# One stage instead of two: merge, output projection, memory keys/values and cross queries

## The chip, the cores and the metric

The kernel runs on one core of one Trainium2 chip. The metric is the device time of one execution in microseconds (us). The kernel before took 2871.36 us (median of 3 runs, 2869.28 to 2875.1). One further execution was taken with the hardware profiler; all rows below are from it.

## The reference, cut to what matters

The reference is one step of a hybrid encoder layer over 1024 prompt tokens and 8 x 16 sample tokens (1152 columns in all, D_MODEL = 1024). The part that is touched:

```python
def rmsnorm(x, g):
    y = x * lax.rsqrt(jnp.mean(x * x, axis=-1, keepdims=True) + 1e-6)
    return y * g

x = x + W_out(sum_b sigmoid(gate_b) * (branch_b @ W_branch_b))     # three branches, 512 -> 1024 each
k, v = split(rmsnorm(mem, norm_mem) @ w_mem_kv, 2)                 # 256 memory rows, 1024 -> 2048
q = rmsnorm(x, norm_x) @ w_xq                                      # 1152 columns, 1024 -> 1024
s = q . k / 16;  x = x + softmax(s) @ v @ w_xo                     # 4 heads of 256
```

Afterwards comes a gated ConvFFN and a final rmsnorm. The memory keys and values (`o_mem`) are outputs too. The RMS factor belongs to a column (a token or a memory row), the gain `g` to a feature, so `(x * g * r) @ W` equals `((x * g) @ W) * r`.

## The kernel before, in words

All activations lie transposed: a feature on a partition, 8 rows of 128 features (`KD`), tokens along the free axis, T = 1152 in three chunks of TC = 384. The program is a chain of stages: in-projection, LRU, RWKV, `stage_merge`, `stage_queries`, `stage_cross`, `stage_tail`. Each is a `with Stage(...)` that owns its buffers, its eight PSUM banks and its semaphores; its exit clears the semaphores and puts a barrier on all engines, so nothing of the next stage starts ahead of it. Within a stage each engine has its own program in a fixed order, written out by hand, and semaphores join them.

**A product** (class `Product`, lines 115 to 307) multiplies by a weight matrix, one tile of 128 output features after another, in pairs (slot `s` = 0, 1). To keep precision each operand is split in a rounded part (`hi`, fp32r) and a rest (`lo`), and three matmuls are added: hi*hi, lo*hi, hi*lo. One tile with 1152 columns is so 8 rows x 3 passes x 3 chunks = 72 matmuls of 384 columns; one of the memory product is 8 x 3 = 24 matmuls of 256 columns. For tile j, SP loads the weights into `raw[s]` once `rest` says that the slot's earlier tile has been split (lines 146, 152). ACT makes `hi` (`split_hi`, L174), which waits for the weights and for `ready` of the tile two before. DVE makes `lo` (`split_lo`, L179). PE runs the tile (L252; the first tile of a product L272) when `lo` is there and the slot's PSUM banks have been emptied (`used`). `pipeline` gives ACT and DVE their order: split of tile 2p, evacuation of tile 2p-1, split of 2p+1, evacuation of 2p. With `after=` the weight buffers are handed from one product to the next; with `next_split` the next product's first two weight tiles are split in the course of this one's last ones. `after_tile=` calls a function on PE behind each tile.

**stage_merge** (L1744): three branch products of half depth (36 matmuls a tile), whose results DVE multiplies with the gates and sums in `xt` (L1853, L1855, L1857); POOL loads the gates (L1792), ACT does the sigmoid (L1820) and rounds the sum (L1814), DVE its rest (L1839). Then `out`, the output projection: SP loads the residual rows into `xt` (L1783) and DVE adds each result to them (L1740). ACT has only the weight splits to do in `out`.

**stage_queries** (L1876): SP loads the memory and the first weights after the barrier. `Norm` (class at L310) of the memory: ACT squares (L342), PE sums over the partitions with a matrix of ones (L365, plain fp32), ACT takes the root (L349), DVE the reciprocal (L372), then for each piece DVE multiplies by gain and factor (L379), ACT rounds (L358), DVE takes the rest (L389). Then `pm`, 16 tiles of K/V, DVE copies them out (L1934). Then the same `Norm` on `xt` in three chunks, and `pq`, 8 tiles of queries; its first tile goes chunk by chunk so as to follow the norm. ACT copies the results out (L1920) and stores them in DRAM (L1922).

**stage_cross** (L1949) begins with 16 transposes of V (L2086) and the load of `q` from DRAM (L1984), for which its first scores (L2024) wait.

Of the kernel before, what the change touches and what calls it, by code (L numbers as in the profile page):

```python
# [26 lines left out]
TC = 384  # L27
# [9 lines left out]
NMEM = 256  # L37
XH, XHD = 4, 256
EPS = 1e-6
GN_EPS = 64e-5  # L40
DEC = float(np.exp(-0.5))

# [44 lines left out]
class Stage:  # L87
# [15 lines left out]
    def sb(self, name, shape, dt=F32):  # L103
        return self.ctx.enter_context(self.nc.sbuf_tensor(f"{self.name}_{name}", shape, dt))
# [10 lines left out]
class Product:  # L115
# [121 lines left out]
    def products(self, pe, x_rest, by_chunk, beside=None, freed=None, after_row=None, after_tile=None):  # L237
# [42 lines left out]
        if after_tile:  # L280
            after_tile(1)
            for p in range(1, self.pairs):
                for s in range(2):
                    tile(p, s, True)
                    after_tile(2 * p + s)
            return
        if not beside:
# [1456 lines left out]
def stage_merge(nc, env, io):  # L1744
# [3 lines left out]
    with Stage(nc, "merge") as st:  # L1748
        banks = st.banks()
        S = st.sem  # L1750
        xt = env["xt"]
        operands = [st.sb(f"operands{i}", [P, KD, T], F32R) for i in range(2)]
        bh, bl = [x[:, 0:KM] for x in operands], [x[:, KM:KD] for x in operands]
        total = xt
        xh, xl = operands[1], st.sb("merged_lo", [P, KD, T], F32R)
        ring = st.sb("branch", [P, 3, T])
        gates = [st.sb(f"gate{s}", [P, T]) for s in range(2)]
        tmp = st.sb("gated", [P, NTC, TC])
# [5 lines left out]
        out = Product(st, "wout", KD, KD // 2, wtile(io["w_out"], KD), xh, xl, banks, bufs=bufs, after=prods[2])  # L1764
        splits = [StreamSplit(st, f"br{n}", lambda k, n=n: io["branch"][n, :, k], bh[n % 2], bl[n % 2], KM, ring) for n in range(3)]
        half = KD // 2
        with nc.Block() as block:
            @block.sync
            def _(sp):
                for n in range(3):  # L1770
                    prods[n].load_first(sp)
                    if n == 0:
                        splits[0].load(sp)
                    if n < 2:
                        if n:
                            sp.wait_ge(prods[0].ready, KD * NTC)
                        sp.wait_ge(splits[n].rest, KM)
# [6 lines left out]
                out.load_rest(sp)  # L1784

            @block.gpsimd
            def _(pool):
                for n in range(3):
                    def load(p, s, wait=True):
                        if wait:  # L1790
                            pool.wait_ge(prods[n].used, (p * 2 + (s - 1)) * NTC)
                        pool.dma_start(gates[s][:], io["z"][bass.ds(p * 2 + (Z_G + n * KD + s), 1)].rearrange("o p t -> (o p) t")).then_inc(S(f"gate_in{n}_{s}"), 16)  # L1792
                    for s in range(2):
                        if n:
                            pool.wait_ge(prods[n - 1].used, (KD - 1 + s) * NTC)
                        load(0, s, False)
                    with pool.Fori(1, half) as p:
                        load(p, 0)
                        load(p, 1)

            @block.scalar
            def _(act):
# [19 lines left out]
                            round_row(p * 2 + (s - 1))  # L1822
                    prods[n].pipeline(act, prods[n].split_hi, gate, next_split=(prods[n + 1] if n < 2 else out).split_hi)
                round_row(KD - 1)
                out.pipeline(act, out.split_hi, lambda p, s: None)

            @block.vector
            def _(dve):
# [38 lines left out]
                out.pipeline(dve, out.split_lo, add_to_residual(dve, out, xt, None))  # L1867

            @block.tensor
            def _(pe):  # L1870
                for n in range(3):
                    prods[n].products(pe, splits[n].rest, False)
                out.products(pe, S("x_rest"), False)


def stage_queries(nc, env, io):  # L1876

    with Stage(nc, "xq") as st:
        banks = st.banks()
        S = st.sem  # L1880
        xt, vec = env["xt"], env["vec"]
        xh, xl = st.sb("xh", [P, KD, T], F32R), st.sb("xl", [P, KD, T], F32R)
        mem = st.sb("mem", [P, KD, NMEM])
        out = [st.sb(f"q{s}", [P, T]) for s in range(2)]
        bufs, nbufs = Product.buffers(st, KD, "w"), Norm.buffers(st, "norm")
        ones = env["mask"]("ones")
        nx = Norm(st, "nx", xt, vec[:, VAT["norm_x"]:], xh, xl, ones, banks, bufs=nbufs)
        nm = Norm(st, "nm", mem, vec[:, VAT["norm_mem"]:], xh, xl, ones, banks, tc=NMEM, ntc=1, bufs=nbufs)
        nx.eps = nm.eps = env["eps"]
        pq = Product(st, "wq", KD, KD // 2, wtile(io["w_xq"], KD), xh, xl, banks, bufs=bufs)  # L1890
        pm = Product(st, "wm", KD, KD, wtile(io["w_mem_kv"], KD), xh, xl, banks[6:8], tc=NMEM, ntc=1, bufs=bufs)
        kv = env["kv"]
        with nc.Block() as block:
            @block.sync
            def _(sp):
                sp.dma_start(mem[:], io["memt"]).then_inc(S("mem_in"), 16)
                pm.load(sp)
                sp.wait_ge(pm.rest, 2 * KD)
                pq.load_first(sp)
                sp.wait_ge(pm.used, 2 * KD)  # L1900
                sp.dma_start(io["o_mem"], kv[:]).then_inc(S("kv_stored"), 16)
                pq.load_rest(sp)
                sp.wait_ge(S("kv_stored"), 16)

            @block.scalar
            def _(act):
                act.wait_ge(S("mem_in"), 16)
                pm.first_splits(act, pm.split_hi)
                nm.scalar(act)
                pm.pipeline(act, pm.split_hi, lambda p, s: None)  # L1910
                act.wait_ge(pm.ready, 2 * KD)
                nx.squares(act, weights=pq)
                nx.roots(act)

                def evac(p, s):
                    if not (isinstance(p, int) and p == 0):
                        act.wait_ge(S(f"q_stored{s}"), p * 16)
                    for c in range(NTC):
                        act.wait_ge(pq.ready, (p * 2 + s) * NTC + (c + 1))
                        act.copy(out[s][:, c * TC:(c + 1) * TC], pq.bank[s][c][:, 0:TC]).then_inc(pq.used, 1)  # L1920
                    act.wait_ge(pq.used, (p * 2 + (s + 1)) * NTC)
                    act.dma_start(io["q"][:, bass.ds(p * 2 + s, 1)].rearrange("p o t -> p (o t)"), out[s][:]).then_inc(S(f"q_stored{s}"), 16)  # L1922
                pq.pipeline(act, pq.split_hi, evac)
                for s in range(2):
                    act.wait_ge(S(f"q_stored{s}"), 16 * pq.pairs)

            @block.vector
            def _(dve):
                pm.first_splits(dve, pm.split_lo)
                nm.vector(dve)  # L1930

                def evac(p, s):
                    dve.wait_ge(pm.ready, p * 2 + (s + 1))
                    dve.tensor_copy(kv[:, bass.ds(p * 2 + s, 1)].rearrange("p o t -> p (o t)"), pm.bank[s][0][:, 0:NMEM]).then_inc(pm.used, 1)  # L1934
                pm.pipeline(dve, pm.split_lo, evac)
                pq.first_splits(dve, pq.split_lo)
                nx.vector(dve)
                pq.pipeline(dve, pq.split_lo, lambda p, s: None)

            @block.tensor  # L1940
            def _(pe):
                nm.tensor(pe)
                pm.products(pe, nm.rest, True)
                pe.wait_ge(nm.rooted, 1)
                nx.tensor(pe)
                pq.products(pe, nx.rest, True)


def stage_cross(nc, env, io):  # L1949
# [576 lines left out]
def hybrid_stream_step(nc, io):  # L2526
    for name, shape in SCRATCH.items():
        io[name] = nc.dram_tensor(f"scratch_{name}", shape, F32, kind="Internal").ap() if name not in io else io[name]
    with ExitStack() as ctx:
# [7 lines left out]
        for stage in (stage_in_projection, stage_lru, stage_rwkv):  # L2537
            stage(nc, env, io)
        env["xt"] = sb("xt", [P, KD, T])
        stage_merge(nc, env, io)  # L2540
        with nc.sbuf_tensor("mem_kv", [P, 2 * KD, NMEM], F32) as kv:
            env["kv"] = kv
            stage_queries(nc, env, io)
            stage_cross(nc, env, io)
        stage_tail(nc, env, io)


# [75 lines left out]
```

## Time and profile before

| what | value |
|---|---|
| median of 3 runs | 2871.36 us |
| the profiled execution, its own time | 2877.42 us |
| its span, first to last instruction | 2875.9 us |
| PE matmul busy | 2592.2 us (90%) |
| DVE busy | 1340.6 us (47%) |
| ACT busy | 745.6 us (26%) |
| POOL busy | 223.1 us (8%) |
| mean granted TensorE clock | 0.946 |

Start of the span is 0. `stage_merge` has its first matmul at 1267.3 us; `out`, its last product, ends with the matmuls that start at 1538.50 us; `stage_queries` lies from there to 1753.7. A profile's busy time of PE counts matmuls that overlap; where the pace matters, the distance of their starts is read. "idle before" in a row is the engine's idle time ahead of the row, with what ended it.

### The profile page before, as it was taken

To read this page: it belongs to the slowest core of one execution; us is meant where nothing else is said; L and a number is where in the kernel's file an instruction comes from. 1 tells how busy PE (TensorE), PEld (TensorE's weight loads), DVE (VectorE), ACT (ScalarE), POOL (GpSimd) and SP (SyncE) were. 2 spreads that over 40 slices of the span, in tenths; PEclk is the share of its full clock that TensorE was granted. 3 is DMA by queue.
4 is the path that set the end of the run, shared out by engine and by line. 5 is a ranking of instruction groups with operands and counts; after the bars stand their busy time and mean duration, and the time that the engine had idled before them with its cause. 6 is when DMAs were issued, how large, how long until landed. Compare 5 with 4: busy or idle time off the path is not lost. (4 is left out here: it accounts for less than half of the span.)

```text
span 2875.9 us, 49184 instructions
## 1 busy us (share of the span) xinstructions
PE 2592.2 (90%) x20376; PEld 2466.1 (86%) x20376; DVE 1340.6 (47%) x2044; ACT 745.6 (26%) x1147; POOL 223.1 (8%) x373
## 2 busy tenths in 40 slices
PE   6999999999648889839997897879999999999996
PEld 4999999999537778729997696779999999989995
DVE  5102334431566777434723612435665556553256
ACT  4111122221434444123412422323111111111122
POOL 0001110000222233110000000000000000000000
PEclk9999999999759999869998999989999999999998
DMA  3222233322530100034421316431111111123233
GB/s 129 86 85 93 86 104 110 109 96 80 128 127 28 32 23 23 9 127 157 152 96 69 121 71 240 144 130 37 44 47 59 68 68 68 68 97 104 66 95 123
DMA packets 138016, 258.85 MB, mean 90 GB/s; under 512 B 43440, under 2 KB 86240, under 8 KB 135056
## 3 DMA queue, kind: packets, MB, share of 16 engines
q1 hardware_dynamic: 103248, 185.30, 19.3%
q0 software_dynamic: 9168, 37.75, 4.0%
q10 hardware_dynamic: 25472, 33.95, 3.2%
q8 instruction: 98, 1.61, 0.2%
q14 instruction: 30, 0.25, 0.0%
HBM read 190.36 MB, written 67.52 MB: 90 GB/s over the span
## 5 line engine op out<-in xcount | busy, mean ns | idle before, releaser
L252 PE MATMUL tail_bank<-tail_x_hi,tail_w_hi 128*128 128x384 f32 x1494 | 359.7, 340 | 8.2 <-DVE tail_w_lo L179 8.2
L252 PE MATMUL tail_bank<-tail_x_lo,tail_w_hi 128*128 128x384 f32 x1494 | 358.4, 339 | 0.0
L252 PE MATMUL tail_bank<-tail_x_hi,tail_w_lo 128*128 128x384 f32 x1494 | 358.3, 339 | 0.0
L252 PE MATMUL inproj_bank<-inproj_xh,inproj_win_hi 128*128 128x384 f32 x1224 | 283.2, 340 | 0.0
L252 PEld LDWEIGHTS tail_bank<-tail_x_hi,tail_w_hi 128*128 128x128 f32 x1494 | 270.8, 189 | 11.8 <-DVE tail_w_lo L179 11.3
L252 PE MATMUL inproj_bank<-inproj_xl,inproj_win_hi 128*128 128x384 f32 x1224 | 278.8, 336 | 0.0
L252 PE MATMUL inproj_bank<-inproj_xh,inproj_win_lo 128*128 128x384 f32 x1224 | 278.7, 336 | 0.0
L252 PEld LDWEIGHTS tail_bank<-tail_x_hi,tail_w_lo 128*128 128x128 f32 x1494 | 270.9, 189 | 0.0
L252 PEld LDWEIGHTS tail_bank<-tail_x_lo,tail_w_hi 128*128 128x128 f32 x1494 | 270.7, 188 | 0.0
L252 PEld LDWEIGHTS inproj_bank<-inproj_xh,inproj_win_hi 128*128 128x128 f32 x1224 | 216.2, 189 | 2.7 <-issue 2.7
L252 PEld LDWEIGHTS inproj_bank<-inproj_xh,inproj_win_lo 128*128 128x128 f32 x1224 | 218.2, 188 | 0.0
L252 PEld LDWEIGHTS inproj_bank<-inproj_xl,inproj_win_hi 128*128 128x128 f32 x1224 | 218.2, 188 | 0.0
L174 ACT CAST tail_w_hi<-tail_w_raw 128x1024 fp32r<-128x1024 f32 (+2 forms) x100 | 92.6, 926 | 473.7 <-PE tail_bank L252 325.5
L179 DVE TENSOR_TENSOR inproj_win_lo<-inproj_win_raw,inproj_win_hi 128x1024 fp32r<-128x1024 f32 x52 | 63.5, 1224 | 250.1 <-ACT inproj_win_hi L174 250.1
L252 PE MATMUL merge_bank<-merge_operands,merge_w_hi 128*128 128x384 f32 x672 | 143.5, 341 | 13.6 <-DVE merge_w_lo L179 13.6
L2417 DVE TENSOR_TENSOR tail_room<-tail_bank,tail_rs 128x384 f32<-128x384 f32 x132 | 59.6, 507 | 181.7 <-PE tail_bank L252 181.4
L252 PEld LDWEIGHTS merge_bank<-merge_operands,merge_w_hi 128*128 128x128 f32 x672 | 121.6, 193 | 14.2 <-DVE xt L1853 8.9
L179 DVE TENSOR_TENSOR tail_w_lo<-tail_w_raw,tail_w_hi 128x1024 fp32r<-128x1024 f32 (+2 forms) x100 | 107.0, 1070 | 56.1 <-ACT tail_w_hi L174 56.0
L1740 DVE TENSOR_TENSOR xt<-tail_bank,xt 128x384 f32<-128x384 f32 x96 | 47.9, 551 | 168.4 <-PE tail_bank L252 155.9
L687 ACT COPY inproj_z<-inproj_bank 128x384 f32<-128x384 f32 x114 | 47.7, 497 | 201.9 <-PE inproj_bank L252 201.2
L252 PE MATMUL merge_bank<-merge_operands,merge_w_lo 128*128 128x384 f32 x420 | 97.3, 340 | 0.0
L252 PEld LDWEIGHTS merge_bank<-merge_operands,merge_w_lo 128*128 128x128 f32 x420 | 76.6, 192 | 0.0
(379 smaller groups left out, 4135.1 us busy)
## 6 DMA issues: line engine op xcount, KB each, us to landing
inproj_win_raw<-in_w_in SPq DMA_DIRECT2D x52, 512.0 KB, 3.5
tail_w_raw<-in_w_up SPq DMA_DIRECT2D x44, 512.0 KB, 4.3
scratch_z<-inproj_z ACTq DMA_DIRECT2D x38, 576.0 KB, 2.8
merge_gate<-scratch_z POOLq DMA_DIRECT2D x24, 576.0 KB, 4.0
scratch_h<-tail_room SPq DMA_DIRECT2D x18, 576.0 KB, 3.1
tail_room<-scratch_h POOLq DMA_DIRECT2D x18, 576.0 KB, 4.2
tail_w_raw<-in_w_down SPq DMA_DIRECT2D x24, 384.0 KB, 3.1
xq_w_raw<-in_w_mem_kv SPq DMA_DIRECT2D x16, 512.0 KB, 3.2
```

The source lines that it names most:

```text
L174: act.copy(self.hi[s][:, 0:self.kt], self.raw[s][:, 0:self.kt]).then_inc(self.rounded, 1)
L179: dve.tensor_tensor(self.lo[s][:, 0:self.kt], self.raw[s][:, 0:self.kt], self.hi[s][:, 0:self.kt].bitcast(F32), ALU.subtract).then_inc(sel ...
L252: mm = pe.matmul(self.bank[s][c][:, 0:self.tc], w[s][:, k, :], x[:, k, c * self.tc:(c + 1) * self.tc], start=(k == 0 and n == 0), stop=last)
L687: act.copy(out[s][:, c * TC:(c + 1) * TC], prod.bank[s][c][:, 0:TC]).then_inc(prod.used, 1)
L1740: dve.tensor_tensor(row, prod.bank[s][c][:, 0:TC], row, ALU.add).then_inc(prod.used, 1)
L2417: dve.tensor_tensor(u[s][:, 2 + c * TC:2 + c * TC + n], up.bank[s][c][:, 0:n], rs[:, c * TC:c * TC + n], ALU.mult).then_inc(S(f"u{s}"), 1)
```

## The change

`stage_queries` goes; its two products `pm` and `pq` follow `out` inside `stage_merge`, with the same weight buffers. The RMS factor is no longer applied to the operands: x * gain is rounded and split, and the factor is multiplied when DVE takes a result from PSUM. The sums of squares are added up over the 8 rows on DVE before PE sums over the partitions: one fp32 matmul for the memory, three for `xt`. The order of each engine:

- POOL loads the memory (1 MB) into the idle branch ring after the gates of branch 1. It also stores the queries, in place of ACT.
- ACT, at `out`'s tile 0: 8 rounded memory rows (128x256) and two squares (128x1024). After each tile i of `out`, the square of row i (128x1152). In `pm`: the last square at tile 0; the three roots at tile 3; the rounding of x rows 0 to 6 at the even tiles from 2 on, row 7 at tile 15.
- DVE, at `out`'s tile 0: 8 memory rests, two reductions of 4 rows each, one add. From tile 2 on one sum of squares (128x1152) for each tile. In `pm`: two such sums, a multiply for each tile, the three reciprocals of 128x384 behind tile 5 (ahead of the split of tile 7), 8 rests of x rows.
- PE: one fp32 matmul behind `out`'s tile 1, three behind `pm`'s tile 3. No barrier between the two parts.
- The K/V tile and one operand buffer get fixed addresses at the end of SBUF; the memory's hi and lo parts lie in the other half of that operand buffer.

```diff
+        pm = Product(st, "wm", KD, KD, wtile(io["w_mem_kv"], KD), memh, meml, banks[6:8], tc=NMEM, ntc=1, bufs=bufs, after=out)
+        pq = Product(st, "wq", KD, KD // 2, wtile(io["w_xq"], KD), xh, xl, banks, bufs=bufs, after=pm)
...
+        sq, acc, rs = gates, ring[:, 2], tmp[:].rearrange("p c t -> p (c t)")
...
             @block.sync
...
                 out.load_rest(sp)
+                pm.load(sp)
+                pq.load_first(sp)
+                sp.wait_ge(pm.used, 2 * KD)
+                sp.dma_start(io["o_mem"], kv[:]).then_inc(S("kv_stored"), 16)
+                pq.load_rest(sp)
...
             @block.gpsimd
...
+                    if n == 1:
+                        pool.wait_ge(splits[2].rest, KM)
+                        pool.dma_start(mem, io["memt"]).then_inc(S("mem_in"), 16)
+
+                def store(p, s):
+                    pool.wait_ge(pq.used, (p * 2 + (s + 1)) * NTC)
+                    pool.dma_start(io["q"][:, bass.ds(p * 2 + s, 1)].rearrange("p o t -> p (o t)"), gates[s][:]).then_inc(S(f"q_stored{s}"), 16)
...
             @block.scalar
...
-                out.pipeline(act, out.split_hi, lambda p, s: None)
...
+                def square(i):
+                    act.wait_ge(out.used, (i + 1) * NTC)
...
+                    act.activation(sq[i % 2][:] if i else acc, xt[:, i], ACT.Square).then_inc(S("squared"), 1)
...
+                out.pipeline(act, out.split_hi, beside_out, next_split=pm.split_hi, unrolled=out.pairs)
+                pm.pipeline(act, pm.split_hi, beside_mem, next_split=pq.split_hi, unrolled=pm.pairs)
+                pq.pipeline(act, pq.split_hi, lambda p, s: None)
             @block.vector
...
+                def sum_row(i):
+                    dve.wait_ge(S("squared"), i + 1)
...
+                    dve.tensor_tensor(acc, acc, sq[i % 2][:], ALU.add).then_inc(S("row_summed"), 1)
...
+                def rest_x(k):
+                    dve.wait_ge(S("xq_rounded"), k + 1)
+                    dve.scalar_tensor_tensor(out=xl[:, k], in0=xt[:, k], scalar=gain("norm_x", k), in1=xh[:, k].bitcast(F32),
+                                             op0=ALU.mult, op1=ALU.subtract).then_inc(S("xq_rest"), 1)
...
+                def beside_mem(p, s):
+                    i = 2 * p + s
+                    if i == 0:
+                        sum_row(KD - 1)
+                        dve.wait_ge(S("mem_inverse"), 1)
+                    dve.wait_ge(pm.ready, i + 1)
+                    dve.tensor_tensor(kv[:, i], pm.bank[s][0][:, 0:NMEM], rs_mem[:], ALU.mult).then_inc(pm.used, 1)
+                    if i == 5:
+                        for c in range(NTC):
+                            dve.wait_ge(S("rooted"), c + 1)
+                            dve.reciprocal(rs[:, chunk(c)], rs[:, chunk(c)]).then_inc(S("inverse"), 1)
+                    elif i and i % 2 == 0:
+                        rest_x(i // 2 - 1)
+                    elif i == 2 * KD - 1:
+                        rest_x(KD - 1)
+
+                def scale_q(p, s):
...
+                    for c in range(NTC):
+                        dve.wait_ge(pq.ready, (p * 2 + s) * NTC + (c + 1))
+                        dve.tensor_tensor(gates[s][:, chunk(c)], pq.bank[s][c][:, 0:TC], rs[:, chunk(c)], ALU.mult).then_inc(pq.used, 1)
...
             @block.tensor
...
-                out.products(pe, S("x_rest"), False)
+                out.products(pe, S("x_rest"), False, freed=S("slot_free"), after_tile=mem_sum)
+                pe.wait_ge(S("mem_rooted"), 1)
+                pm.products(pe, S("mem_rest"), False, after_tile=row_sums)
+                pe.wait_ge(S("rooted"), NTC)
+                pq.products(pe, S("xq_rest"), False)
-def stage_queries(nc, env, io):
...
```

## Rows read from the trace of the kernel before

**Rows 1.** The page: busy time of each engine, its share and its instructions.
```profile
PE 2592.2 (90%) x20376; PEld 2466.1 (86%) x20376; DVE 1340.6 (47%) x2044; ACT 745.6 (26%) x1147; POOL 223.1 (8%) x373
```

**Rows 2.** Windows; columns: stretch, length, busy of PE, PEld, DVE, ACT, POOL, clock, DMA.
```profile
1453.00:1540.00 87.00, 86.19 (x498) 85.87 (x496) 17.07 (x27) 5.74 (x6) 0.00 (x0) 1.00 0.08 24
```

**Rows 3.** Timeline of PE, 1538 to 1761: start, duration, line, operation, count, [idle before].
```profile
1538.50 0.69 PE L252 MATMUL merge_bank<-merge_merged_lo,merge_w_hi 128*128 128x384 f32 x3
1550.16 6.66 PE L365 MATMUL xq_bank<-xq_norm_sq,masks 128*128 128x256 f32 x16 [10.97 <-ACT xq_norm_sq L342]
1571.08 0.28 PE L252 MATMUL xq_bank<-xq_xl,xq_w_hi 128*128 128x256 f32 x1
1571.20 0.28 PE L252 MATMUL xq_bank<-xq_xh,xq_w_hi 128*128 128x256 f32 x1
...
1612.37 5.40 PE L365 MATMUL xq_bank<-xq_norm_sq,masks 128*128 128x384 f32 x16 [0.70 <-ACT xq_norm_sq L342]
1748.12 0.69 PE L252 MATMUL xq_bank<-xq_xl,xq_w_hi 128*128 128x384 f32 x3
1753.71 3.37 PE L2086 MATMUL cross_bank<-masks,mem_kv 128*128 128x128 f32 x16 [4.91 <-PEq L100]
1760.59 1.71 PE L2024 MATMUL cross_bank<-mem_kv,cross_q 128*128 128x256 f32 x4 [3.51 <-DMA cross_q<-scratch_q]
```

**Rows 4.** Timeline of PE around an idle stretch in the merge stage.
```profile
1349.11 1.32 PE L252 MATMUL merge_bank<-merge_operands,merge_w_hi 128*128 128x384 f32 x3 [5.04 <-DVE merge_w_lo L179]
1353.11 1.16 PE L252 MATMUL merge_bank<-merge_operands,merge_w_lo 128*128 128x384 f32 x3
1354.07 1.54 PE L252 MATMUL merge_bank<-merge_operands,merge_w_hi 128*128 128x384 f32 x6
1355.45 0.69 PE L252 MATMUL merge_bank<-merge_operands,merge_w_lo 128*128 128x384 f32 x3
1355.98 1.20 PE L252 MATMUL merge_bank<-merge_operands,merge_w_hi 128*128 128x384 f32 x6
```

**Rows 5.** Groups of DVE, 1440 to 1761: count, busy, mean ns, idle before.
```profile
L179 DVE TENSOR_TENSOR xq_w_lo<-xq_w_raw,xq_w_hi 128x1024 fp32r<-128x1024 f32 x24 | 29.3, 1225 | 81.4 <-ACT xq_w_hi L174 81.4
L379 DVE SCALAR_TENSOR_TENSOR xq_norm_xn<-xt,vec,xq_norm_rs 128x384 f32<-128x384 f32 x24 | 14.8, 619 | 0.8
L372 DVE RECIPROCAL xq_norm_rs<-xq_norm_rs 128x384 f32<-128x384 f32 x3 | 7.6, 2547 | 2.9 <-ACT xq_norm_rs L349 2.9
L379 DVE SCALAR_TENSOR_TENSOR xq_norm_xn<-xq_mem,vec,xq_norm_rs 128x256 f32<-128x256 f32 x8 | 3.8, 484 | 0.2
L1839 DVE TENSOR_TENSOR merge_merged_lo<-xt,merge_operands 128x1152 fp32r<-128x1152 f32 x2 | 2.7, 1350 | 0.0
L1934 DVE COPY mem_kv<-xq_bank 128x256 f32<-128x256 f32 x4 | 1.7, 424 | 5.7 <-PE xq_bank L252 4.5 <-PE xq_bank L272 1.2
```

**Rows 6.** Timeline of DVE: the start of `out`, and a reduction in the cross stage.
```profile
1443.59 1.22 DVE L179 TENSOR_TENSOR merge_w_lo<-merge_w_raw,merge_w_hi 128x1024 fp32r<-128x1024 f32 x1
1444.73 1.35 DVE L1839 TENSOR_TENSOR merge_merged_lo<-xt,merge_operands 128x1152 fp32r<-128x1152 f32 x1
1450.89 1.53 DVE L1740 TENSOR_TENSOR xt<-merge_bank,xt 128x384 f32<-128x384 f32 x3 [4.81 <-PE merge_bank L272]
...
1766.01 1.29 DVE L2168 TENSOR_REDUCE cross_stat<-cross_bank 128x2 f32<-128x512 f32 x2 [38.30 <-PE cross_bank L2024]
```

**Rows 7.** Timeline of ACT: a rounding, a weight split and a gate's sigmoid.
```profile
1396.37 1.26 ACT L1820 ACTIVATE merge_gate<-merge_gate,vec 128x1152 f32<-128x1152 f32 x1
1442.44 1.16 ACT L1814 CAST merge_operands<-xt 128x1152 fp32r<-128x1152 f32 x1 [1.95 <-DVE xt L1857]
1452.41 1.05 ACT L174 CAST merge_w_hi<-merge_w_raw 128x1024 fp32r<-128x1024 f32 x1 [8.81 <-DMA merge_w_raw<-in_w_out]
```

**Rows 8.** DMA issues of the page: engine, count, KB each, median us to landing.
```profile
merge_gate<-scratch_z POOLq DMA_DIRECT2D x24, 576.0 KB, 4.0
xq_w_raw<-in_w_mem_kv SPq DMA_DIRECT2D x16, 512.0 KB, 3.2
scratch_q<-xq_q ACTq DMA_DIRECT2D x8, 576.0 KB, 2.8
```

More of the change, by code:

```diff
@@ L283, in products @@
                 for s in range(2):
-                    tile(p, s, True)
+                    tile(p, s, True, freed=freed if p == self.pairs - 1 and s == 1 else None)
                     after_tile(2 * p + s)
@@ L1751, in stage_merge @@
         xt = env["xt"]
-        operands = [st.sb(f"operands{i}", [P, KD, T], F32R) for i in range(2)]
+        at_top = lambda name, shape, dt, size: nc.alloc_sbuf_tensor_at(f"merge_{name}", shape, dt, offset=SBUF_END - size)
+        operands = [at_top("operands0", [P, KD, T], F32R, 4 * KD * T), st.sb("operands1", [P, KD, T], F32R)]
+        memh = at_top("mem_hi", [P, KD, NMEM], F32R, 4 * KD * T)
+        meml = at_top("mem_lo", [P, KD, NMEM], F32R, 4 * KD * (T - NMEM))
         bh, bl = [x[:, 0:KM] for x in operands], [x[:, KM:KD] for x in operands]
@@ L1755, in stage_merge @@
         xh, xl = operands[1], st.sb("merged_lo", [P, KD, T], F32R)
+        kv, vec, ones = env["kv"], env["vec"], env["mask"]("ones")
+        gain = lambda name, k: vec[:, VAT[name] + k:VAT[name] + k + 1]
+        rs_mem = st.sb("rs_mem", [P, NMEM])
         ring = st.sb("branch", [P, 3, T])
@@ L1799, in _ @@
                         load(p, 1)
+                    if n == 1:
[4 more added lines that the diff above has]
+                    pool.dma_start(io["q"][:, bass.ds(p * 2 + s, 1)].rearrange("p o t -> p (o t)"), gates[s][:]).then_inc(S(f"q_stored{s}"), 16)
+                for p in range(pq.pairs):
+                    store(p, 0)
+                    store(p, 1)
+                for s in range(2):
+                    pool.wait_ge(S(f"q_stored{s}"), 16 * pq.pairs)
             @block.scalar
@@ L1824, in _, with mem_rows @@
                 round_row(KD - 1)
-                out.pipeline(act, out.split_hi, lambda p, s: None)
+                def mem_rows():
+                    act.wait_ge(S("mem_in"), 16)
+                    act.wait_ge(prods[2].ready, KD * NTC)
+                    for k in range(KD):
+                        act.activation(memh[:, k], mem[:, k], ACT.Identity, scale=gain("norm_mem", k)).then_inc(S("mem_rounded"), 1)
+                    act.wait_ge(prods[2].used, KD * NTC)
+                    for n in range(2):
+                        act.activation(mem_sq[n].rearrange("p (k m) -> p k m", k=4), mem[:, 4 * n:4 * n + 4], ACT.Square).then_inc(S("mem_squared"), 1)
@@ new lines, in beside_out @@
+                def beside_out(p, s):
+                    i = 2 * p + s
+                    if i == 0:
+                        mem_rows()
+                    if i == 2:
+                        act.wait_ge(S("mem_sum"), 1)
+                        act.activation(rs_mem[:], banks[7][:, 0:NMEM], ACT.Sqrt, scale=1.0 / D, bias=env["eps"][:, 0:1]).then_inc(S("mem_rooted"), 1)
+                    if i < KD - 1:
+                        square(i)
+                def beside_mem(p, s):
+                    i = 2 * p + s
+                    if i == 0:
+                        square(KD - 1)
+                    elif i == 3:
+                        for c in range(NTC):
+                            act.wait_ge(S("summed"), c + 1)
+                            act.activation(rs[:, chunk(c)], banks[c][:, 0:TC], ACT.Sqrt, scale=1.0 / D, bias=env["eps"][:, 0:1]).then_inc(S("rooted"), 1)
+                    elif i % 2 == 0:
+                        round_x(i // 2 - 1)
+                    elif i == 2 * KD - 1:
+                        round_x(KD - 1)
@@ L1866, in _, with mem_rows @@
                 dve.wait_ge(S("residual_in"), 16 * KD)
-                out.pipeline(dve, out.split_lo, add_to_residual(dve, out, xt, None))
+                add_out = add_to_residual(dve, out, xt, None)
+                def mem_rows():
+                    for k in range(KD):
+                        dve.wait_ge(S("mem_rounded"), k + 1)
+                        dve.scalar_tensor_tensor(out=meml[:, k], in0=mem[:, k], scalar=gain("norm_mem", k), in1=memh[:, k].bitcast(F32),
+                                                 op0=ALU.mult, op1=ALU.subtract).then_inc(S("mem_rest"), 1)
+                    for n in range(2):
+                        dve.wait_ge(S("mem_squared"), n + 1)
+                        dve.tensor_reduce(tmp[:, n, 0:NMEM], mem_sq[n].rearrange("p (k m) -> p m k", k=4), AX.X, ALU.add).then_inc(S("mem_summed"), 1)
+                    dve.wait_ge(S("mem_summed"), 2)
+                    dve.tensor_tensor(tmp[:, 2, 0:NMEM], tmp[:, 0, 0:NMEM], tmp[:, 1, 0:NMEM], ALU.add).then_inc(S("mem_summed"), 1)
@@ new lines, in scale_q @@
+                def scale_q(p, s):
+                    first = isinstance(p, int) and p == 0
+                    if not first:
+                        dve.wait_ge(S(f"q_stored{s}"), p * 16)
+                    elif s == 0:
+                        dve.wait_ge(S("inverse"), NTC)
+                        dve.wait_ge(S("row_summed"), KD - 1)
+                    for c in range(NTC):
+                        dve.wait_ge(pq.ready, (p * 2 + s) * NTC + (c + 1))
+                        dve.tensor_tensor(gates[s][:, chunk(c)], pq.bank[s][c][:, 0:TC], rs[:, chunk(c)], ALU.mult).then_inc(pq.used, 1)
@@ L1869, in _ @@
+                out.pipeline(dve, out.split_lo, beside_out, next_split=pm.split_lo, unrolled=out.pairs)
+                pm.pipeline(dve, pm.split_lo, beside_mem, next_split=pq.split_lo, unrolled=pm.pairs)
+                pq.pipeline(dve, pq.split_lo, scale_q)
             @block.tensor
@@ L1872, in _ @@
                     prods[n].products(pe, splits[n].rest, False)
-                out.products(pe, S("x_rest"), False)
-def stage_queries(nc, env, io):
[L1878 to L1946, printed above, removed]
@@ new lines, in mem_sum, with row_sums @@
+                def mem_sum(i):
+                    if i == 1:
+                        pe.wait_ge(S("mem_summed"), 3)
+                        pe.matmul(banks[7][:, 0:NMEM], ones, tmp[:, 2, 0:NMEM], start=True, stop=True).then_inc(S("mem_sum"), 1)
+                def row_sums(i):
+                    if i == 3:
+                        pe.wait_ge(S("row_summed"), KD - 1)
+                        for c in range(NTC):
+                            pe.matmul(banks[c][:, 0:TC], ones, acc[:, chunk(c)], start=True, stop=True).then_inc(S("summed"), 1)
@@ L2539, in hybrid_stream_step @@
         env["xt"] = sb("xt", [P, KD, T])
+        env["kv"] = nc.alloc_sbuf_tensor_at("mem_kv", [P, 2 * KD, NMEM], F32, offset=SBUF_END - 4 * 2 * KD * NMEM)
         stage_merge(nc, env, io)
[L2541 to L2544, printed above, removed]
+        stage_cross(nc, env, io)
         stage_tail(nc, env, io)
```

29 lines of the change are left out of this document (added).

## The prediction

> **What bounds the kernel now.** I read the page first: PE's matmuls are busy 90% of the span, DVE 47% [rows 1]. PE is the bound, so a change gains what PE idles or runs slowly, and costs what it adds to PE or makes PE wait for. The windows come next: over `out` PE is busy 86.2 of 87.0 us at full clock, while DVE has 17.1 us of work and ACT is lower still [rows 2]. That is empty room beside PE. Then PE's timeline [rows 3]. `out` ends at 1538.50 + 0.69 = 1539.2. PE idles 10.97 us (barrier, memory and weights loading, first squares) and then sums squares for the memory; the last query matmul ends at 1748.12 + 0.69 = 1748.8. From end to end: 209.6 us.
>
> What would PE need for the products alone? Two 256-column matmuls start 1571.20 - 1571.08 = 0.12 us apart [rows 3]; 16 tiles x 24 x 0.12 = 46.1 us. With 384 columns I take the pace from `out`: DVE's first residual add starts at 1450.9 [rows 6], when the first tile's first chunk is ready, six matmuls (1.0) before the tile's end at 1451.9; the seven other tiles end at 1539.2, so a tile takes 87.3 / 7 = 12.47 us and a matmul 12.47 / 72 = 0.173. The queries' 8 tiles: 99.8 us. Together 145.9. So 63.7 us of the 209.6 are waiting, norm sums and half-speed matmuls. That is the most the change can give.
>
> **The change part by part.**
>
> *Merge products.* The memory load is one more DMA on POOL's queue, behind the last gate of branch 1 and ahead of the first of branch 2. 576 KB of gate land in 4.0 us [rows 8], so 1 MB takes about 7. The next gate is issued some 5 us later, so it may be about 2 us late; the sigmoid started at 1396.37 and takes 1.26 [rows 7], and its result is wanted only after the first 6.2 us tile of branch 2. I take 0; bounds 0 and 3 us. Below nothing there is no reason.
>
> *`out`, first tile.* This is the tightest place of the first half, because the next weight split stands behind new work on both engines. DVE waits for all residual rows; they have landed by 1450.9, where the first residual add waited for PE and no DMA [rows 6]. Then: 8 memory rests at about 0.41 (0.484 long each, overlapping 0.08) [rows 5] = 3.3; two reductions over 1024 elements, each like the two of 512 in 1.29 [rows 6], = 2.6; an add with its waits 0.6; the residual add 1.5 [rows 6]. That makes 1458.9. ACT squares row 0 in about 1.2 (1.16 for a rounding of that size) and splits the weights in 1.05 [rows 7]; DVE's split takes 1.22 [rows 5]: 1462.4. PE wants these for tile 2, six tiles before `out`'s end: 1539.2 - 6 x 12.47 = 1464.4. Slack 2.0 us: cost 0. Bounds: 0, and 3 if the reductions, which read with a stride that no row shows, take twice as long. The later tiles add a square (1.2) and a sum (1.35) to some 4 us of work in 12.5: hidden. PE gets one fp32 matmul of 256 columns: 16 records, which are 8 matmuls of 384, take 5.40 us [rows 3], so 0.68 each and 0.5 for this.
>
> *The hand-over to K/V.* The first weights are split under `out`'s last tile. The second tile's weights come late: at 1539.2 DVE has the last residual add (1.5), a sum of squares (1.3) and then the split (1.2), so about 1543.3, while PE wants it after the first memory tile, 2.9 us long: 1.2 us of stall. The next sum delays a further split by 0.3. I take 1.5; bounds 0.5 and 5 (the idle that a split brought in the merge stage was 5.04 [rows 4]).
>
> *K/V tiles.* DVE now carries: 16 splits x 1.22 = 19.5; 16 multiplies at 0.42 (as the copy) = 6.7; two sums 2.7; three reciprocals 7.6; 8 x rests of 1152 columns. The rest isn't in the trace; the same operation takes 0.484 at 256 and 0.619 at 384 [rows 5], 1.05 ns an element, so 1.42 (bounds 1.35, the plain subtraction of that width [rows 5], and 1.8, three of 384 at 0.619): 11.4. Sum 48 us beside 46 of PE. So the places are what counts:
> - Three sums with ones on PE behind tile 3: 3 x 0.68 = 2.0, with gaps 2.2. ACT's roots (0.56 each) keep up beside them; 0.15 more.
> - The reciprocals stand behind tile 5's multiply and ahead of tile 7's split. Tile 5 ends; multiply 0.4, reciprocals 7.5, split 1.2, signals 0.2: 9.3 us, while tile 6 covers 3.0. PE idles 6.3 us. Bounds 5 and 8.
> - An even tile's end starts multiply 0.42, x rest 1.4, split 1.2, signals 0.1: 3.1 to 3.2 against 2.88 of the tile beside it: 0.25 each for the some four pairs that aren't covered otherwise: 1.0. Bounds 0 and 4 (rests of 1.8, weights landing later than 3.2 [rows 8]). The weights' own ring, 3.2 to land, 1.05 and 1.22 to split, is 5.5 to 5.9 a pair against 5.76 and stays even.
> - After idling 5.04 us PE ran at half speed, starts 0.32 apart, from 1349.11 to about 1354.8, and at full speed by 1355.45 [rows 4]. Behind my stall of 6.3 the same is due: 5.7 us at 0.32 / 0.173 = 1.85 times the time, a loss of 2.6. Bounds 0 and 19 (below).
> - Entering the queries, a split behind x row 6's rest: 0.3.
>
> *Queries.* The operands are there, the first tile doesn't follow a norm, DVE's scaling of 3 x 0.5 lies under the next tile as ACT's copies did: 99.8 us, nothing added. The K/V output's store lies under it.
>
> *The end.* Before, PE stopped at 1748.8, the store landed 2.8 after its issue [rows 8], and the cross stage's PE began at 1753.7, its scores at 1760.6 [rows 3]. The store now goes by POOL's queue, whose loads of that size take 4.0 [rows 8]: +1.2; bounds 0 and 3. The cross stage is otherwise moved as it is.
>
> *Sum.* 0.5 + 145.9 + 1.5 + 2.35 + 6.3 + 1.0 + 2.6 + 0.3 = 160.5 for what took 209.6: 49.1 less. With the end's 1.2: 47.9 less. The profiled execution took 2877.4 (1.5 beside its span), so its like would take 2829.5. The median of the runs is 6.1 lower, and the forecast for it is 2871.4 - 47.9 = 2823.5.
>
> **A rule against this change.** DVE takes most of the new work. In the rows a split starts at 1443.59, lasts 1.22, and the next instruction starts at 1444.73, 0.08 before that ends [rows 6]: the recorded durations are the whole price. The Trainium skill says otherwise ("VectorE: DVE Perf Modes", section "The DRAIN you can't avoid"): each Vector instruction is followed by a flush of about its duration less 266 ns, which the next one can't skip. The traces speak against it, unless the flush lies within the recorded durations. As a rival, from rows: if each DVE instruction held its follower for as long again, DVE's 48 us would be 96, the K/V part 96 in place of about 60, and the gain 12: 2859.
>
> **The rivals.**
> - *Hand-overs that stall.* That weights are handed on within a stage doesn't secure PE: the merge stage, which does the same, has a 5.04 us wait for a split, with half speed after it [rows 4]. For: twice more such a change of products here, with DVE fuller. Against: here the first splits of the next product stand under a 12.5 us tile. Two of 5.0 with 2.6 of slow matmuls each, less my 1.8: +13, 2837.
> - *Low clock through K/V.* The rest of K/V after the stall, 9 tiles, all at the lower of the two levels: 9 x 2.88 x 0.85 = 22, less 2.6: +19, 2843. For: PE has short waits there every other tile. Against: at half speed a tile is 5.3 us long, longer than DVE's 3.2, so PE doesn't wait and works as densely as after 1349.
> - *Slower than before.* The same mechanism, in its full size: the granted level stays low on into the queries. Each us spent low loses 0.46 us of work, so the gain of 48 is gone after 105 us low and the kernel is clearly slower from about 117. The remaining 26 us of K/V and 99.8 of queries would last 22 + 85 = 107 us longer, 104 beyond my 2.6: 2927. Against: both the wait of 5.04 and the longer ones were over in some 6 us of work [rows 4].
> - *Less stall than I count.* Reciprocals hidden better, no half-speed stretch, hand-overs clean: 2.6 + 1.5 + 1.0 + 1.2 = 6 less, 2817.
>
> **How the numbers follow.** Forecast 2823.5, within 2818 to 2831: 0.70. Less stall: 0.09. Hand-overs: 0.09. Low clock in K/V: 0.07. Held-up DVE: 0.01. Slower: 0.03; the last 0.01 for no change. The range takes in the small bounds and most of the hand-over case: 2814 to 2838. About 0.2% is what a measurement of this kernel can tell from none. Faster 0.96, same 0.01, slower 0.03.
>
> **What would show it.** In the changed profile: no PE idle over 2 us between `out` and the tile behind the reciprocals; there one of about 6.3 released by DVE's weight split, then starts 0.21 apart for 256 columns for some 6 us; K/V from `out`'s end to the first query matmul about 60 us; 99.8 us of queries without a wait. Wrong would be: a PE wait at `out`'s third tile (reductions slow), K/V tiles 3.5 us or more apart throughout (DVE instructions dearer), low clock in the queries, or more than 6 us between the last query matmul and the cross stage's first.

## The result and the profile after

The changed kernel takes 2832.77 us (median of 4 runs, 2830.82 to 2835.45) against 2873.23 for the one before in the same comparison (4 runs): ratio 0.986, 95% interval 0.9846 to 0.9874, 36 to 44 us less. A second comparison (5 runs against 9) gave 2828.43 against 2873.63: 0.9847 (0.9834 to 0.9861). The forecast was 2823.5, 47.9 us less, with 2814 to 2838 as its range. The profiled execution took 2832.27 us, 45.2 less than that of before.

The page's busy times, to be read beside [rows 1]. PE's fell by 32.9 us and its matmul records by 56; since the span got shorter too, its share is 90% as before. DVE's and POOL's rose by under 4 us, ACT's fell by 16:

```profile
PE 2559.3 (90%) x20320; PEld 2447.7 (86%) x20320; DVE 1344.4 (47%) x2030; ACT 729.4 (26%) x1085; POOL 226.9 (8%) x382
```

Windows of the changed kernel, columns as in [rows 2]: most of `out`, then K/V, then the queries.

```profile
1453.00:1540.00 87.00, 87.00 (x503) 86.95 (x502) 34.32 (x45) 16.49 (x16) 0.00 (x0) 1.00 0.15 50
1542.30:1600.90 58.60, 51.12 (x391) 48.70 (x390) 45.02 (x47) 28.89 (x28) 0.00 (x0) 0.94 0.41 135
1600.90:1701.00 100.10, 100.08 (x576) 99.78 (x576) 20.60 (x31) 7.38 (x7) 3.73 (x7) 1.00 0.26 94
```

DVE's work under `out` doubled, from 17.1 to 34.3 us, and PE is busy all 87 us: PE never waited for that work. K/V lasts 58.6 us for 46.1 of matmuls (384 at 0.12), and the queries run without a break. PE's timeline, to be read beside [rows 3]:

```profile
1541.63 0.68 PE L253 MATMUL merge_bank<-merge_merged_lo,merge_w_hi 128*128 128x384 f32 x3
1542.15 0.28 PE L273 MATMUL merge_bank<-merge_mem_hi,merge_w_hi 128*128 128x256 f32 x1
...
1545.94 0.38 PE L253 MATMUL merge_bank<-merge_mem_hi,merge_w_hi 128*128 128x256 f32 x1 [0.80 <-DVE merge_w_lo L180]
...
1554.93 2.10 PE L2025 MATMUL merge_bank<-merge_branch,masks 128*128 128x384 f32 x6
...
1571.88 0.58 PE L253 MATMUL merge_bank<-merge_mem_hi,merge_w_hi 128*128 128x256 f32 x1 [5.94 <-DVE merge_w_lo L180]
...
1573.33 0.41 PE L253 MATMUL merge_bank<-merge_mem_hi,merge_w_hi 128*128 128x256 f32 x1
1573.54 0.41 PE L253 MATMUL merge_bank<-merge_mem_hi,merge_w_lo 128*128 128x256 f32 x1
...
1576.64 0.28 PE L253 MATMUL merge_bank<-merge_mem_hi,merge_w_hi 128*128 128x256 f32 x1
1576.76 0.28 PE L253 MATMUL merge_bank<-merge_mem_hi,merge_w_lo 128*128 128x256 f32 x1
...
1600.91 0.41 PE L273 MATMUL merge_bank<-merge_operands,merge_w_hi 128*128 128x384 f32 x1 [0.19 <-issue]
...
1700.31 0.69 PE L253 MATMUL merge_bank<-merge_merged_lo,merge_w_hi 128*128 128x384 f32 x3
1710.24 3.73 PE L2172 MATMUL cross_bank<-masks,mem_kv 128*128 128x128 f32 x16 [9.24 <-PEq L101]
```

The 10.97 us of idle behind `out` are gone; the first K/V matmul starts 0.5 us after `out`'s last group. In K/V there is one long wait, of 5.94 us, and behind it matmuls 0.21 us apart until about 1575.9, then 0.12. The granted clock in these two windows shows the same: first the lower of its two levels (0.50 of full speed, 1.2 of 2.4 GHz), then the upper one. It had fallen at about 1569.1, while PE idled.

```profile
1571.88:1575.89 4.01, 4.01 (x19) 4.01 (x20) 2.73 (x3) 0.00 (x0) 0.00 (x0) 0.50 0.42 141
1575.89:1580.00 4.11, 4.11 (x36) 4.11 (x36) 1.97 (x3) 2.48 (x3) 0.00 (x0) 0.99 0.35 118
```

From `out`'s end (1542.3) to the last query matmul's (1701.0) it is 158.7 us, where it was 209.6. But ahead of the cross stage PE now idles 9.24 us where it idled 4.91.

Not all that went was waiting. The kernel before had PE sum the squares of all 8 rows: 64 records, the two groups of [rows 3] (6.66 and 5.40 us) and this one:

```profile
1618.11 10.59 PE L365 MATMUL xq_bank<-xq_norm_sq,masks 128*128 128x384 f32 x32 [0.34 <-ACT xq_norm_sq L342]
```

Together 22.65 us. The changed kernel has 8 such records, about 0.4 us under `out` and the 2.1 at 1554.93. So some 20 of the 50.9 us between 209.6 and 158.7 are matmuls that DVE's additions made needless; the rest is idle time and slow matmuls.

DVE's timeline shows the two reductions, dearer than they were priced, a K/V multiply with the reciprocals right behind it, and the weight split that PE waits for:

```profile
1456.14 3.87 DVE L1955 TENSOR_REDUCE merge_gated<-merge_gate 128x256 f32<-128x1024 f32 x2
...
1563.04 0.42 DVE L1987 TENSOR_TENSOR mem_kv<-merge_bank,merge_rs_mem 128x256 f32<-128x256 f32 x1 [0.26 <-PE merge_bank L253]
1563.38 7.37 DVE L1991 RECIPROCAL merge_gated<-merge_gated 128x384 f32<-128x384 f32 x3
1570.66 1.16 DVE L180 TENSOR_TENSOR merge_w_lo<-merge_w_raw,merge_w_hi 128x1024 fp32r<-128x1024 f32 x1
```

### The profile page after: what moved, and what is told of

Its sections match the earlier page's. It is cut to its first block and busy times, and to the rows that moved or that the text cites. A ratio compares the mean times of both kernels' runs of the same rounds, so it can differ in the third digit from the quotient of the medians.

```text
span 2830.7 us, 48844 instructions
## 1 busy us (share of the span) xinstructions
PE 2559.3 (90%) x20320; PEld 2447.7 (86%) x20320; DVE 1344.4 (47%) x2030; ACT 729.4 (26%) x1085; POOL 226.9 (8%) x382
## 5 line engine op out<-in xcount | busy, mean ns | idle before, releaser
L253 PE MATMUL merge_bank<-merge_operands,merge_w_hi 128*128 128x384 f32 x840 | 181.9, 340 | 13.5 <-DVE merge_w_lo L180 13.5
L253 PEld LDWEIGHTS merge_bank<-merge_operands,merge_w_hi 128*128 128x128 f32 x840 | 151.7, 192 | 14.2 <-DVE xt L1932 8.9
L253 PE MATMUL merge_bank<-merge_operands,merge_w_lo 128*128 128x384 f32 x588 | 135.4, 338 | 0.0
L1741 DVE TENSOR_TENSOR xt<-tail_bank,xt 128x384 f32<-128x384 f32 x96 | 47.9, 551 | 168.5 <-PE tail_bank L253 155.9
L253 PEld LDWEIGHTS merge_bank<-merge_operands,merge_w_lo 128*128 128x128 f32 x588 | 106.5, 191 | 0.0
```

Source lines behind the costliest of these rows:

```text
L253: mm = pe.matmul(self.bank[s][c][:, 0:self.tc], w[s][:, k, :], x[:, k, c * self.tc:(c + 1) * self.tc], start=(k == 0 and n == 0), stop=last)
L1741: dve.tensor_tensor(row, prod.bank[s][c][:, 0:TC], row, ALU.add).then_inc(prod.used, 1)
```

## The experiments

All edits are to the changed kernel, unless said otherwise. Whole executions of one kernel scatter by 4 to 14 us, so beside medians I use the time in the profile from the merge stage's first matmul to the cross stage's first: 486.4 and 483.8 us in two profiles of the kernel before, 440.6 and 439.2 in two of the changed one: 45.2 apart. Where the part up to K/V is the same, a steadier measure is the time from K/V's first matmul to the cross stage's first: 168.1 us in both profiles of the changed kernel. The kernel before took 214.7 and 214.3 from the same place, 0.52 us after `out`'s last group of matmuls starts.

**Both kernels again.**

> The changed kernel once more, unaltered, in 5 rounds against the one before, to tighten the ratio of 0.986 (0.9846 to 0.9874). The two profiled executions differ by 45.2 us, the medians by 40.5. Theory: the change is worth about 45 (50 in the stage, less 4 at its end), and the rest is scatter of other stages: ratio 0.984 to 0.986. Rival: something outside the changed stage got slower for good, by 3 to 5 us, and the RWKV part before it, 2.3 us longer in the first profile, is the place: it is longer by 2 or more here too.

> The kernel before, unaltered, one look with a profile. Its merge stage began at 1267.3 us in the first profile, that of the changed kernel at 1269.6. Theory (scatter of the RWKV part): another start here, off by 1 us or more from 1267.3. Rival (the change moved something ahead of it): 1267.3 again within 0.5.

The merge stage began at 1270.5 us here and at 1265.5 in the new profile of before; over 13 profiles of both kernels and the variants below, with the same instructions up to there, it lies anywhere from 1264.1 to 1271.7. By its own sign the rival held in this run, 3.2 us later than 1267.3; what speaks against it is the nine variants, which have the change and the same instructions ahead of the stage and start at 1267.3 us on average. The 2.3 us are best read as scatter: nothing ahead of the stage got slower for good that these profiles can tell. Nor does anything behind it: from the cross stage's first matmul to the end of the span it is 1122.2 and 1125.4 us in the profiles of before, 1120.5 and 1117.2 in those of the changed kernel.

**Late reciprocals.**

```diff
-                    if i == 5:
-                        for c in range(NTC): ... dve.reciprocal(...)
...
+                for c in range(NTC):
+                    dve.wait_ge(S("rooted"), c + 1)
+                    dve.reciprocal(rs[:, chunk(c)], rs[:, chunk(c)]).then_inc(S("inverse"), 1)
                 pq.pipeline(dve, pq.split_lo, scale_q)
```

> The three reciprocals of 7.4 us move from behind K/V tile 5 to DVE's idle stretch under the first query tile (8.7 us long). Theory: they alone cause the PE stall of 5.94 us and the slow matmuls after it (a tile of 4.9 in place of 2.9): 8 us faster than the changed kernel, and no PE idle over 1 us in K/V. Rival (DVE's total of 48 us bounds K/V): the load of the other instructions fills the room, so 2 us or less.

2822.2 us (2816.14 to 2827.98), 6.2 below the changed kernel in the same comparison. DVE's timeline in this kernel, and then the window of K/V:

```profile
1598.42 7.37 DVE L2007 RECIPROCAL merge_gated<-merge_gated 128x384 f32<-128x384 f32 x3
1607.19 1.50 DVE L2002 TENSOR_TENSOR merge_gate<-merge_bank,merge_gated 128x384 f32<-128x384 f32 x3 [1.40 <-PE merge_bank L273]
```

```profile
1544.10:1595.30 51.20, 49.58 (x391) 47.05 (x389) 38.03 (x44) 28.89 (x28) 0.00 (x0) 1.00 0.47 155
```

K/V lasts 51.2 us in place of 58.6 and holds the full clock throughout (1.00); DVE is even idle 1.40 us before the first query result. From K/V's first matmul to the cross stage's first it is 160.6 us, 7.5 less. So 7.4 us come from the reciprocals: 5.94 of stall and the slow matmuls. The edit also takes their 7.4 us out of DVE's load in K/V (38.0 us in place of 45.0), so by itself it doesn't tell their place from their length; that DVE's total isn't the bound is shown by the last experiment, where 11 us more leave K/V and it gets 0.2 us shorter.

**Stores by ACT, and the last two by ACT.**

```diff
-                    pool.wait_ge(pq.used, ...); pool.dma_start(io["q"]...)       # POOL, all eight
+                    act.wait_ge(pq.used, ...); act.dma_start(io["q"]...)         # act_store: all eight; last_two_act: the last two
```

> The queries' stores are issued by ACT again instead of POOL. In the changed kernel POOL's DRAIN behind its last store takes 2.7 us after that store has landed, and the barrier comes 3.1 us after the landing. Theory: the drain belongs to software DMA and goes with it: PE's idle ahead of the cross stage falls from 9.2 to about 5, 4 us faster. Rival: the larger stage with its more semaphores makes the exit longer, whoever stores: 8 us of idle or more stay, under 1 us faster.

> POOL issues the first six stores of queries as in the changed kernel, ACT the last two. Theory (the drain is a fixed price paid when POOL reaches the stage's end after software DMAs): it is paid under the last PE tiles, so as with all stores on ACT the barrier follows the landing within 1 us, 4 us faster. Rival (the length comes from the count of POOL's DMAs or the landing of the slower queue): no faster than the changed kernel by more than 1 us.

2822.89 us (2821.72 to 2829.24), 5.5 below the changed kernel; the mixed one 2826.99 (2819.28 to 2832.04), in a comparison where the one before stood at 2877.69: ratio 0.9837 (0.9819 to 0.9855), by medians not to be told from the changed kernel. The profiles decide: from merge to cross it is 434.7 and 434.4 us, 5.2 and 5.5 less than the changed kernel. Of that, 1.3 and 1.8 us lie ahead of K/V, which the edit doesn't touch; from K/V's first matmul on it is 164.1 and 164.4 us in place of 168.1: 4.0 and 3.7 less, as the theory had it. The ends of the two stages, first the changed kernel's, where POOL's DRAIN (an instruction of the stage's exit that each engine has) begins 3.3 us after the last store's issue (1702.53) and all others wait for it:

```profile
L1780 POOLq DRAIN  x1: 2746/2746/2746, 1705.8 to 1705.8; - x1
L1780 SPq EVENT_SEMAPHORE  x1: 17/17/17, 1708.7 to 1708.7; - x1
```

Then the mixed kernel's:

```profile
L1780 POOLq DRAIN  x1: 2582/2582/2582, 1672.7 to 1672.7; - x1
...
L1780 ACTq DRAIN  x1: 8/8/8, 1697.2 to 1697.2; - x1
L1780 SPq EVENT_SEMAPHORE  x1: 17/17/17, 1697.4 to 1697.4; - x1
```

and its PE, the last query group and the cross stage's first; last, the cross stage's first with all stores on ACT:

```profile
1692.28 0.69 PE L253 MATMUL merge_bank<-merge_merged_lo,merge_w_hi 128*128 128x384 f32 x3
1698.79 1.51 PE L2178 MATMUL cross_bank<-masks,mem_kv 128*128 128x128 f32 x6 [5.82 <-PEq L101]
```

```profile
1699.71 1.51 PE L2170 MATMUL cross_bank<-masks,mem_kv 128*128 128x128 f32 x6 [5.54 <-PEq L101]
```

The drain is as long there (2.58 us) but runs at 1672.7, under PE's work, and PE's idle falls to 5.82; with all stores on ACT it is 5.54. So POOL pays it after its last DMA, and it counts only where POOL is the last to arrive. That its length is fixed isn't shown: these kernels differ by only two of POOL's stores, and the drain that POOL began in the merge stage of the kernel before, 0.1 us after issuing its last load, took 4.73 us (hidden). Some 0.6 to 0.9 over the old 4.91 stay; the rival with the larger stage has part of that: from the barrier's first signals (the SPq rows above) to PE's start it is 1.4 us in the mixed kernel and 1.1 with all stores on ACT, where it was 0.7 before.

**The memory's norm in the open.**

```diff
-                    if i == 0:
-                        mem_rows()
...
+                square(KD - 1)
+                mem_rows()
+                act.wait_ge(S("mem_sum"), 1)
+                act.activation(rs_mem[:], ..., ACT.Sqrt, ...)
                 pm.pipeline(act, pm.split_hi, beside_mem, ...)
```

(and the same for DVE and PE)

> One part undone: the memory's rounding, squares, sums, root and reciprocal stand between the output projection and K/V in place of under the projection's first tiles; everything else as in the changed kernel. Theory: what the stage gains is mostly such work put under PE; exposed, it costs PE about 14 us of idle (squares and sum of the last x row, 3.3 of rests, 3.9 of reductions, sum, root) and 2.5 of slow matmuls: 14 to 17 us slower than the changed kernel. Rival: what was gained there is the barrier and the first loads, not the norm: 6 us or less slower.

2842.93 us (2837.38 to 2851.1, 4 runs), ratio to before 0.9892 (0.9867 to 0.9918); merge to cross 453.2 us, 13.3 more than the changed kernel. PE's timeline of it:

```profile
1550.68 1.22 PE L2012 MATMUL merge_bank<-merge_gated,masks 128*128 128x256 f32 x2 [12.11 <-DVE merge_gated L1952]
1552.46 0.58 PE L273 MATMUL merge_bank<-merge_mem_hi,merge_w_hi 128*128 128x256 f32 x1 [0.56 <-ACT merge_rs_mem L1897]
...
1553.27 0.41 PE L273 MATMUL merge_bank<-merge_mem_hi,merge_w_hi 128*128 128x256 f32 x1
```

With no barrier and the weights there, this small norm, behind the last x row's square and sum (1.35 us on DVE, at 1542.06), costs PE 12.7 us of idle. From K/V's first matmul on this kernel takes 168.1 us like the changed one, so all of the loss lies ahead of it. The theory expected 14 to 17 and was a little high; the rival's 6 is out.

**All three edits, and two of them.** The third edit takes each x row's rest behind the next weight split:

```diff
+                    if i % 2 and i > 1:
+                        rest_x((i - 3) // 2)
                     dve.wait_ge(pm.ready, i + 1)
...
-                    elif i and i % 2 == 0:
-                        rest_x(i // 2 - 1)
```

> Both together, and the rest of each x row is taken behind the next weight split instead of ahead of it (which in the changed kernel makes a pair of K/V tiles 6.1 us long instead of 5.8). Theory: 8 + 4 + 1.5 = 13 us faster than the changed kernel. If DVE's load bounds K/V: 5 to 6.

> The reciprocals under the first query tile and the stores on ACT, but each x row's rest still ahead of the weight split. Theory: 12 us faster than the changed kernel, and about 1.5 slower than with the rests behind the split.

> The version with all three edits once more, in the same call as the one without the third. The first time the medians were 2816.5 and 2813.1 in different calls, while their profiles have K/V at 50.4 and 50.6 us. Theory: the rest's place is worth 0.2 us, so the two agree within 2 us here.

> Late reciprocals and stores by ACT once more: 10 to 12 us faster than the changed kernel (2828 to 2833), ratio to the one before about 0.980.

With all three: 2816.53 and 2816.15 us, ratios to before 0.9804 (0.979 to 0.9817) and 0.9794 (0.9777 to 0.9811). With two: 2813.09 and 2818.97, ratios 0.9785 (0.9766 to 0.9803) and 0.9815 (0.9802 to 0.9829). The third edit was expected to give 1.5 us; whole executions can't tell it: in one comparison the two differ by 2.8 us, within their ranges. The profiles put it under 1 us: from K/V's first matmul to its last the two take 50.4 and 50.6 us (50.2 and 50.7 the second time), and to the cross stage's first 156.1 and 156.7 (155.9 and 156.8). Why so little shows in ACT's weight splits of the kernel with three edits:

```profile
1568.74 1.05 ACT L175 CAST merge_w_hi<-merge_w_raw 128x1024 fp32r<-128x1024 f32 x1 [2.51 <-DMA merge_w_raw<-in_w_mem_kv]
...
1574.78 1.05 ACT L175 CAST merge_w_hi<-merge_w_raw 128x1024 fp32r<-128x1024 f32 x1 [2.52 <-DMA merge_w_raw<-in_w_mem_kv]
```

Every other split waits for its weights, and a pair lasts 5.9 to 6.0 us: buffer freed, 3.5 to land, 1.05 and 1.22 to split. The rest was in the way of one slot; the ring of two weight buffers bounds the other just above the 5.76 of the matmuls. That is read from these rows; no run had a third buffer.

Both versions are faster than both kernels: three edits are 11.9 us below the changed kernel in the comparison that had the two, and 2% below the one before.

**The x rows between K/V and the queries**, built on the version with two edits:

```diff
-                    elif i % 2 == 0:
-                        round_x(i // 2 - 1)
...
+                for k in range(KD):
+                    round_x(k)
```

> On top of the version with late reciprocals and stores by ACT: the rounding of the x rows and their rests also leave the K/V tiles and stand between K/V and the queries, as an unnormalised copy of what the kernel before did there. Theory: K/V hides this work nearly whole; outside, PE waits for the first row's rest only (signals, weight split, 1.2 + 1.4: 3.8 us) and then follows row by row, with up to 2 us of slow matmuls, while K/V gets about 0.5 shorter: 3.5 to 5.5 us slower than the version it is built on. Rival (11 us of DVE work cost K/V as much as they would in the open): no slower, or faster.

2822.43 us (2818.81 to 2826.76), 3.5 above its base in the same comparison. The profiles say more: merge to cross 436.0 us against the base's 429.2 and 427.0, and from K/V's first matmul to the cross stage's first 164.1 against 156.7 and 156.8, 7.4 more where 3.5 to 5.5 was expected. PE waits 5.80 us there, not 3.8:

```profile
1592.52 0.66 PE L273 MATMUL merge_bank<-merge_operands,merge_w_hi 128*128 128x384 f32 x1 [5.80 <-DVE merge_merged_lo L1963]
```

The second query weight split, which stands ahead of the rests on DVE, waited for its weights. The queries then take 102.1 us in place of 100.1. K/V is 50.4 against 50.6. So K/V hides 11 us of rests nearly whole, as expected, and the price in the open was low by 2.

## Why the prediction was right, and what was off

The direction and the mechanism were right, and the median lies in the range of 2814 to 2838, though above the 2818 to 2831 that had most of the weight (the second comparison's 2828.4 lies in it). One of the signs that it named for being wrong did appear: over 6 us, in fact 9.24, between the last query matmul and the cross stage's first (its own 4.91 + 1.2 made 6.1). By the steps of the sum, forecast and then measured in the first profile after:

| step | forecast us | measured us |
|---|---|---|
| PE wait at `out`'s third tile | 0 | 0 |
| memory sum on PE | 0.5 | about 0.4 |
| hand-over to K/V | 1.5 | 0.80 |
| three sums, roots | 2.35 | 2.1 |
| stall behind the reciprocals | 6.3 | 5.94 |
| slow matmuls behind it | 2.6 | 1.7 (4.0 us at 0.21 instead of 0.12) |
| pairs, entry of the queries | 1.3 | 2.0 (the rest of the 58.6) |
| queries | 99.8 | 100.1 |
| end, more than before | 1.2 | 4.3 |

From `out`'s end on the forecast was 160.0 and the measurement 158.7, in part by luck: the stall, the slow matmuls and the hand-over came out shorter, the pairs with the entry of the queries longer. The one step that was mis-sized by more than its bounds is *the end*. It priced the store by POOL's queue at the difference in landing (4.0 against 2.8). The landing was in fact 3.0, so 0.2 of the 1.2 was there. What was missing is POOL's own drain of 2.75 us, which starts behind that landing and holds the barrier, and a slower exit of the larger stage: from the barrier's first signals (1708.7) to PE's start (1710.24) 1.5 us, where it was 0.7. The step's upper bound of 3 was passed too: it counted the transfer and nothing that the issuing engine does after it.

*`out`, first tile* came out right with a wrong part: the two strided reductions take 3.87 us where 2.6 was forecast, half way to the upper bound. Of the slack of 2.0 us, 1.8 was left even so: the split for the third tile ended at 1465.26 and PE began that tile at 1467.08, since other parts of the chain were shorter or earlier than forecast. PE didn't wait.

Of the rivals, *hand-overs that stall* didn't happen (0.80 us). *Low clock through K/V* and the *slower* rival are out: the lower level (granted 0.50) ended after 4.0 us of matmuls, and with the reciprocals moved it didn't occur in K/V at all. The rival that rests on the Trainium skill ("VectorE: DVE Perf Modes", section "The DRAIN you can't avoid"), 2859 us, is out too: in K/V the three reciprocals, 2.49 to 2.54 each, take 7.37 together, and DVE's 45 us of work fit in 58.6. These rows don't show such a flush beyond the recorded durations.

Of the 9.3 us between 2823.5 and 2832.8, 3.1 are the end, less 1.3 in the stage; 1.9 are the median of before, which stood at 2873.2 with more runs. The remaining 5.6 I can't pin to an instruction. The second comparison has 45.2 us of gain in place of 40.5, and merge to cross, two profiles each, 45.2; with starts of the merge stage scattering over 7 us, sampling can explain it, but that is argued and not shown.

What the account by steps leaves out is where the 63.7 us beyond the products were. The forecast took them as one sum of waiting, norm sums and slow matmuls. That was enough for the time, but 22.65 us of it was PE's own work on norm sums, most of which this change removes rather than hides.

## What to carry to other kernels

Work put under a busy engine is free as long as each piece fits the slack of its place; 13 of the some 45 us are lost again when a norm of 256 columns and one row's sum leave such a place. Add up on an idle engine before the busy one sums: some 20 us are matmuls that are no longer there (read from the rows; no run kept them). A long instruction in the queue ahead of a just-in-time split costs its length even where the engine's total would fit: look for the tile that is long enough to cover it, and put it there. When a DMA moves to another engine's queue, count what that engine must do between its last transfer and the barrier.

## What the runs showed of the hardware

- POOL's DRAIN after its last DMA store took 2.58 to 2.75 us, begun when the store had landed (rows above), and 4.73 in the merge stage of the kernel before, begun at 1430.2 just behind the issue of a load at 1430.11. ACT's took 8 ns behind a landed store, and 0.94 in the changed kernel, where ACT issued none of these stores and came to the end right behind a weight split.
- A sum of 4 x 256 elements with the summed ones 1 KB apart takes 1.93 us on DVE, where a sum of the same 1024 elements with neighbours summed takes 1.21 (L2265, `cross_stat<-cross_scores`, at 1734.39 in the changed kernel): 1.6 times. The first writes 256 results and the second 4, so the stride isn't singled out. The kernel before had such a row of 1.21 too.
- A reciprocal of 384 columns takes 2.49 to 2.55 us on DVE, where a multiply of that width takes about 0.5 (three in 1.50).
- PE ran at the lower of its two levels (granted 0.50) for 4.0 us of matmuls after idling 5.94, for 4.1 after 12.11 (1.22 of norm sum and 2.8 of K/V, with 0.56 idle between), and for some 5.5 after 5.04 [rows 4]: in these three the longer wait didn't bring the longer slow stretch.
